# Reordering y, the gates and the reloads, sharing the opening between ScalarE and VectorE, spreading the FFN gate passes, and moving g by 64 bytes

## What is computed

```
h = x + RMSNorm_post(W_out [GLA(xn) ; SSD(xn)]),  xn = RMSNorm_pre(x)
y = h + RMSNorm_post(ConvFFN(RMSNorm_pre(h)))
D_MODEL = 2048; FFN_DIM = 5632; GLA_HEADS = 4; SSD_HEADS = 16

def _conv_ffn(xn, s_ffn, p):
    u = xn @ p['ffn_w_in']
    u, buf = _causal_dwconv(u, s_ffn, p['ffn_conv_w'], p['ffn_conv_b'])
    a, b = jnp.split(u, 2, axis=-1)
    return (jax.nn.silu(a) * b) @ p['ffn_w_out'], buf.astype(xn.dtype)

# in _mixer, once W_in has made q, k, v, g, lr, z, xbc, dt:
    lg = jax.nn.log_sigmoid((lr @ p['gla_w_gate2'] + p['gla_b_gate']).astype(f32)) / GLA_GATE_NORMALIZER
    ...
    y = y.reshape(B, L, SSD_GROUPS, SSD_WIDTH // SSD_GROUPS) * jax.nn.silu(
        z.reshape(B, L, SSD_GROUPS, SSD_WIDTH // SSD_GROUPS).astype(f32))
    y = _rmsnorm(y, p['ssd_norm'].reshape(SSD_GROUPS, SSD_WIDTH // SSD_GROUPS)).reshape(B, L, SSD_WIDTH)
```

## Time and profile before

| what | us |
| --- | --- |
| median of 3 runs | 2804.49 |
| lowest and highest | 2802.88, 2816.77 |
| the profiled execution's own time | 2808.16 |
| its span, first to last instruction | 2806.4 |
| PE busy in the span | 2719.0 |
| granted TensorE clock, mean | 0.983 |
| opening, input projection and recurrences | about 0 to 960 |
| FFN, 22 blocks | about 1045 to 2760 |

### The profile page before, as it was taken

The page is one execution under the profiler, slowest core; times in us unless marked ns, Lnnn a source line. Parts: engine busy times, 40 slices in busy tenths (PEclk is TensorE's granted clock), DMA queues, the critical chain, the costliest instruction groups (busy, mean ns, idle before and its releaser), DMA issues.

```text
span 2806.4 us, 48458 instructions
## 1 busy us (share of the span) xinstructions
PE 2719.0 (97%) x20078; PEld 2675.7 (95%) x20078; DVE 1280.7 (46%) x1462; ACT 744.0 (27%) x1198; POOL 1077.7 (38%) x466
## 2 busy tenths in 40 slices
PE   7999999899999988999999999999999999999996
PEld 6999999799989977999999999999999999999996
DVE  7544544555126346533443444443344434444436
ACT  3322222423103224322222222222222222222222
POOL 5333222323223345443443434443443434344337
PEclk9999999899999989999999999999999999999998
DMA  4222246412343423222222223222222222222224
GB/s 157 88 82 94 78 163 194 162 60 64 131 164 115 150 68 111 91 77 89 76 88 78 84 83 91 83 76 83 76 88 78 83 83 76 90 88 80 76 85 166
DMA packets 84595, 277.00 MB, mean 99 GB/s; under 512 B 9024, under 2 KB 13760, under 8 KB 83536
## 3 DMA queue, kind: packets, MB, share of 16 engines
q1 hardware_dynamic: 56160, 207.12, 23.7%
q10 hardware_dynamic: 28272, 67.35, 6.7%
HBM read 242.79 MB, written 31.65 MB: 98 GB/s over the span
## 4 chain that ended last, share of the span: by engine, by line
PE 69%; issue 19%; POOL 7%; DVE 4%; ACT 0%; DMA 0%; POOLq 0%; DVEq 0%; ACTq 0%
PE psum_proj L894 26%; PE psum_work L894 18%; PE psum_proj L897 13%; PE psum_work L897 9%; POOL w_lo L354 5%; DVE arena L1813 2%; POOL arena L389 1%; DVE x_lo L1341 1%; PE psum_work L1021 1%; POOL arena L406 1%; DVE x_hi L1339 1%; DVE arena L1836 1%; PE psum_work L1016 0%; POOL arena L397 0%; PE psum_work L981 0%
## 5 line engine op out<-in xcount | busy, mean ns | idle before, releaser
L354 POOL TENSOR_TENSOR w_lo<-raw,w_hi 128x1024 fp32r<-128x1024 f32 x386 | 988.1, 2571 | 1673.9 <-ACT w_hi L416 1673.9
L894 PE MATMUL psum_proj<-x_hi,w_hi 128*128 128x288 f32 (+2 forms) x3104 | 880.3, 302 | 32.2 <-POOL w_lo L354 11.5
L894 PE MATMUL psum_proj<-x_lo,w_hi 128*128 128x288 f32 (+2 forms) x3104 | 891.8, 298 | 0.0
L897 PE MATMUL psum_proj<-x_hi,w_lo 128*128 128x288 f32 (+2 forms) x3104 | 669.5, 297 | 0.0
L894 PEld LDWEIGHTS psum_proj<-x_hi,w_hi 128*128 128x128 f32 x3104 | 597.2, 192 | 51.6 <-issue 23.1
L416 ACT ACTIVATE w_hi<-raw 128x1024 fp32r<-128x1024 f32 x386 | 395.0, 1050 | 793.8 <-PE psum_proj L897 520.2
L894 PEld LDWEIGHTS psum_proj<-x_lo,w_hi 128*128 128x128 f32 x3104 | 594.1, 191 | 2.7 <-issue 1.9
L897 PEld LDWEIGHTS psum_proj<-x_hi,w_lo 128*128 128x128 f32 x3104 | 515.7, 190 | 0.0
L894 PE MATMUL psum_work<-x_lo,w_hi 128*128 128x256 f32 (+1 forms) x1408 | 407.0, 296 | 0.0
L894 PE MATMUL psum_work<-x_hi,w_hi 128*128 128x256 f32 (+1 forms) x1408 | 387.0, 297 | 0.7 <-POOL w_lo L354 0.7
L897 PE MATMUL psum_work<-x_hi,w_lo 128*128 128x256 f32 (+1 forms) x1408 | 302.4, 296 | 0.0
(11 more groups left out here) (298 smaller groups left out, 3267.9 us busy)
## 6 DMA issues: line engine op xcount, KB each, us to landing
raw<-in_weights_dram SPq DMA_DIRECT2D x386, 512.0 KB, 3.5
spill<-tail ACTq DMA_DIRECT2D x24, 288.0 KB, 2.1
arena<-in_xT_dram SPq DMA_DIRECT2D x4, 1152.0 KB, 11.3
y_spill<-arena ACTq DMA_DIRECT2D x4, 1152.0 KB, 9.2
h_spill<-arena ACTq DMA_DIRECT2D x1, 4608.0 KB, 14.5
x_hi<-h_spill ACTq DMA_DIRECT2D x1, 4608.0 KB, 17.5
out_yT_dram<-arena ACTq DMA_DIRECT2D x8, 576.0 KB, 3.6
arena<-in_ssdT_in_dram ACTq DMA_DIRECT2D x8, 512.0 KB, 5.7
```

The source lines that it names most:

```text
L354: nc.gpsimd.tensor_tensor(w_lo[:, slot], raw[:, r], w_hi[:, slot].bitcast(F32), ALU.subtract).then_inc(lo_ready, 1)
L894: nc.tensor.matmul(banks[:, n, 0:b - a], w_hi[:, slot, k], (hi, lo)[part][:, a:b], start=first and part == 0, stop=False)
L897: mm = nc.tensor.matmul(banks[:, n, 0:b - a], w_lo[:, slot, k], hi[:, a:b], start=False, stop=last)
```

## The change

Four parts.

1. **Opening.** ACT makes `x_hi` (with the weight vector as its scale) and then the square, for each slice; DVE makes `x_lo` and adds the squares in pairs; POOL has no part in it beside `weight_lo`. PE sums eight pairs over partitions, and from slice 8 on it also works tile 1, slice by slice behind tile 0. The load of the masks moves behind slice 7, and ACT rounds unit 4 before the root.
2. **y, gates, reloads.** ACT rounds the first half of y before it takes the gate logits and the second half right behind them, all in m = 32. exp and ln stand in m = 33, both low halves go out in m = 34, and in m = 35 the two loads of q and k are issued ahead of the two high halves. DVE's steps of the gates go one half tile earlier.
3. **FFN.** DVE's two taps are parted, and the four steps stand behind down tiles 1, 3, 6 and 9. ACT rounds two weight units before `g_hi`, not after.
4. **Memory.** A tensor `apart` of 64 bytes a partition stands ahead of `tail`, `g_hi` and `g_lo`. They begin at 209,792, a multiple of 128.

```diff
+        sb("apart", [P, 16])
         with nc.sbuf_tensor("tail", [P, 4736], F32) as tail:
...
-        xsum = A(14336, T)
+        xsq = [A(11008 + T * i, T) for i in range(4)]
...
             for kt in range(KT):
+                x = xin[kt // 4][:, kt % 4 * T:(kt % 4 + 1) * T]
                 act.wait_ge(x_in[min(kt // 4, 2)], 32 if kt >= 8 else 16)
-                if kt >= 2:
-                    act.wait_ge(sq_used if kt % 2 else sq_sum, kt // 2)
-                nc.scalar.activation(stage[:, kt % 2], xin[kt // 4][:, kt % 4 * T:(kt % 4 + 1) * T],
-                                     ACT.Square).then_inc(sq_ready, 1)
+                nc.scalar.activation(x_hi[:, kt], x, ACT.Copy, scale=V("mix_pre", kt)).then_inc(x_hi_w, 1)
+                if kt >= 4:
+                    act.wait_ge(sq_used, kt // 2 - 1)
+                nc.scalar.activation(xsq[kt % 4], x, ACT.Square).then_inc(sq_ready, 1)
...
+            def y_high(g):
+                for j in range(4 * g, 4 * g + 4):
+                    act.wait_ge(ymix, j + 1)
+                    nc.scalar.activation(y_hi[:, j], XC[:, j], ACT.Copy).then_inc(yhi, 1)
...
                 if m == GAP_GATE:
-                    gates()
-                if m in (GAP_YNORM + 2, GAP_YNORM + 3):
-                    g = m - GAP_YNORM - 2
                     for j in range(2):
                         act.wait_ge(hs_out[j], 16 * BATCHES // 2)
-                    for j in range(4 * g, 4 * g + 4):
-                        act.wait_ge(ymix, j + 1)
-                        nc.scalar.activation(y_hi[:, j], XC[:, j], ACT.Copy).then_inc(yhi, 1)
-                if m == GAP_YNORM + 3:
-                    y_low_out(0)
+                    y_high(0)
+                    gates()
+                    y_high(1)
+                if m == GAP_GATE + 1:
...
-                    load_over_y(0)
-                    y_high_out(0)
-                    load_over_y(1)
-                    y_high_out(1)
+                if m == GAP_GATE + 3:
+                    for g in range(SG):
+                        load_over_y(g)
+                    for g in range(SG):
+                        y_high_out(g)
...
-            def ffn_down(unit, half_unit):
+            def ffn_down(unit, half_unit, blk, q):
 
                 two_hi(unit, half_unit, 2)
+                high_of(2 * blk + 1, q, 1)
                 two_hi(unit + 2, half_unit + 1, 0)
...
+            for kt in range(KT):
+                pe.wait_ge(x_split, kt + 1)
+                mm = kt_of(0, kt)
+                if kt == 7:
+                    mm.then_inc(units_done, 1)
+                if kt >= 8:
+                    if kt == KT - 1:
+                        mm.then_inc(units_done, 1)
+                    mm = kt_of(1, kt - 8)
                 if kt % 2:
-                    pe.wait_ge(sq_ready, kt + 1)
-                    sum_tokens([stage[:, 1]], 0, sq_used, kt == 1, False)
+                    pe.wait_ge(sq_sum, kt // 2 + 1)
+                    sum_tokens([xsq[(kt - 1) % 4]], 0, sq_used, kt == 1, kt == KT - 1)
...
-                    if d in (1, 4, 7):
-                        block_end(blk, q, (1, 4, 7).index(d))
+                    if d in (1, 3, 6, 9):
+                        block_end(blk, q, (1, 3, 6, 9).index(d))
```

More of the change, by code:

```diff
@@ L357, in _ @@
             weight_lo(0, 0, 0)
[L359 to L366, removed]
+            weight_lo(1, 1, 1)
             def weights_lo(start, stop):
@@ L818, in ffn_up, with high_of @@
                             .then_inc(f_silu, 1)
-                        act.wait_ge(f_prod, pair + 1)
-                        nc.scalar.activation(g_hi[:, q, j // 2], fgate, ACT.Copy).then_inc(f_hi, 1)
-            def ffn_down(unit, half_unit):
+                        if first or j == 1:
+                            high_of(pair, q, j // 2)
+            def high_of(pair, q, i):
+                act.wait_ge(f_prod, pair + 1)
+                nc.scalar.activation(g_hi[:, q, i], fgate, ACT.Copy).then_inc(f_hi, 1)
+            def ffn_down(unit, half_unit, blk, q):
                 two_hi(unit, half_unit, 2)
+                high_of(2 * blk + 1, q, 1)
                 two_hi(unit + 2, half_unit + 1, 0)
@@ L927, in sum_tokens, with kt_of @@
                 mm.then_inc(done, 1)
-            def x_arrives(kt):
-                if kt % 2:
-                    pe.wait_ge(sq_ready, kt + 1)
-                    sum_tokens([stage[:, 1]], 0, sq_used, kt == 1, False)
-                pe.wait_ge(x_split, kt + 1)
-            pe.wait_ge(setup, 2)
-            project(0, 0, 0, 0, before=x_arrives)
-            pe.wait_ge(sq_sum, KT // 2)
-            sum_tokens([xsum], 0, sq_used, False, True)
-            with pe.Fori(0, XBC_TILES // 2) as i:
+            def kt_of(tile, kt):
+                slot = 2 * tile + kt // 8
+                if kt % 8 == 0:
+                    pe.wait_ge(lo_ready, slot + 1)
+                return products(slot, kt % 8, tile, (HALF, 256)[tile], kt == 0, kt == KT - 1, x_hi[:, kt], x_lo[:, kt])
+            pe.wait_ge(setup, 2)
+            pe.wait_ge(taken, 2)
+            for kt in range(KT):
+                pe.wait_ge(x_split, kt + 1)
+                mm = kt_of(0, kt)
+                if kt == 7:
+                    mm.then_inc(units_done, 1)
[3 more added lines that the diff above has]
+                    mm = kt_of(1, kt - 8)
+                if kt % 2:
+                    pe.wait_ge(sq_sum, kt // 2 + 1)
+                    sum_tokens([xsq[(kt - 1) % 4]], 0, sq_used, kt == 1, kt == KT - 1)
+            mm.then_inc(units_done, 1)
+            for kt in range(8, KT):
+                mm = kt_of(1, kt)
+            mm.then_inc(units_done, 1)
+            project(2, 4, 0, 0, 256)
+            with pe.Fori(1, XBC_TILES // 2) as i:
                 pair(i, split=256)
@@ L1342, in _ @@
                     .then_inc(x_split, 1)
+                if kt % 2:
+                    ve.wait_ge(sq_ready, kt + 1)
+                    tt_op(xsq[(kt - 1) % 4], xsq[(kt - 1) % 4], xsq[kt % 4], ALU.add).then_inc(sq_sum, 1)
             ve.wait_ge(masks_in, 16)
```

47 lines of the change are left out of this document (26 added, 21 removed).

## The result

| | us |
| --- | --- |
| before, median of 4 runs | 2809.94 (2802.88 to 2816.77) |
| after, median of 4 runs | 2769.06 (2764.26 to 2770.59) |
| ratio of the times | 0.986, 95% interval 0.9839 to 0.9882 |
| profiled execution, before and after: span | 2806.4 and 2768.2 |

The changed kernel is 1.4% faster. The forecast was 2768.8. One more run of before came with this comparison, so its median is 2809.94 here and not 2804.49; from span to span the gain is 38.2 us, where 35.7 had been summed.

What follows compares the result with a forecast made beforehand. TensorE, busy 2719.0 of 2806.4 us, was taken as the bound, leaving its idle time, lower clock and pace. -7.5 - 9.5 - 8.2 - 10.5 = -35.7 took the median from 2804.5 to 2768.8; range 2761 to 2781.

Steps and rivals of the forecast that it cites:

- Opening: Before tile 2: tile 1's work fills the holes where tile 0 waited for slices; -7.5 us, from -6 to -9.5.
- The root and the reciprocal: Opening, for tile 2's buffer: start at 42.5, end before 48.9, hidden by tile 1's second half; otherwise they would cost 5 us.
- The sum: Opening, the four programs laid against each other: tile 2 at 48.9 us, 8.0 earlier, with some 3 us of DVE waits.
- y, gates, reloads: Gates to first attention step: 10.8 us less, the gates' 2.3 included, less 1.3 for the clock; -9.5, from -5 to -12.5.
- The landing: Both loads of q and k before the first attention step: land at 548 us on the old clock, bounds 542.5 and 551.2.
- the step itself: First attention step: four heads in 1.9 us, PE back at the main matmuls at 550.4 instead of 561.2.
- the 1.3 taken off for the clock: First attention step: 1.3 us of the gain given up, for a clock that may fall in the wait of 2.7 us.
- the gates: Gate logits: ACT rounds four slices of y first, so PE returns to the main matmuls 2.3 us later.
- The low halves: y's low halves: out at 530 us behind exp and ln, landing at 534.6 and about 537.5; the loads wait for these.
- FFN passes: FFN down tiles: parted taps remove the wait in full, 21 x 0.39 us; -8.2, from -6 to -8.5.
- g by 64 bytes: FFN, g at a multiple of 128 bytes: 4224 matmuls 2.5 ns shorter each; -10.5 us, from -9.5 to -11.5.
- The first rival: FFN: the place of g changes nothing, so the sum is -25.2 and the time 2779.3 us; chance 13%.

Runs made afterwards that it cites:

- e5: The kernel before with the opening change alone; 2800.97 us, ratio 0.9976 to the kernel before.
- e12: The changed kernel with 192 bytes instead of 64 ahead of tail and g; 2770.62 us, ratio 0.9889 to the kernel before.
- e14: The changed kernel without the 64 bytes ahead of tail and g; 2779.97 us, ratio 0.993 to the kernel before.
- e6: The kernel before with the y, gates and reloads change alone; 2797.54 us, ratio 0.9971 to the kernel before.
- e10: The changed kernel with y's low halves and the two loads issued one half tile earlier each; 2773.58 us, ratio 0.9874 to the kernel before.
- e4: The kernel before with the FFN change alone (taps parted, g_hi behind two weight units); 2797.55 us, ratio 0.9971 to the kernel before.
- e2: The kernel before with 128 bytes ahead of tail, g_hi and g_lo; 2804.13 us, ratio 0.9996 to the kernel before.
- e3: The kernel before with 64 bytes ahead of the arena, moving gla_ops, tail and g; median 2800.14 us, ratio 0.998; second execution, a single run, 2805.16.
- e13: e3 with three matmuls of 8 columns added at the head of PE's program; 2793.08 us in a single run.
- e1: The kernel before with 64 bytes ahead of tail, g_hi and g_lo alone; 2800.94 us against 2806.62, ratio 0.9972.

## Why the prediction was right, step by step

**Opening, -7.5, measured -8.4.** The trace gives 8.4 in after, 9.1 in e5, and 7.7 to 7.8 in e12 and e14; the mean of e5's runs at full clock 8.4. PE started at 11.86 (11.95 predicted), tile 2 came near 48.4 (48.9). The root and the reciprocal hid as said: the reciprocal ends at 46.8. The sum had some 3 us of waits for DVE behind POOL; behind its first instruction PE waited for `x_lo` once in after, 0.9 us. Of the 8.4 us the sum itself had 8.0, and 0.5 were taken off.

**y, gates, reloads, -9.5, measured -7.2 in the profile, -10.0 to -10.2 in the traces of e6, e12 and e14, and -9.3 +- 1.8 in the runs of e6.** The landing was right. With the 15.9 us added that after was ahead before the gates, its loads land at 548.0 on the old clock (548 predicted), PE arrives at 545.6 (545.3), and the wait is 2.4 us (2.7).

Two terms were mis-sized. The first is the step itself: the prediction has PE back at the main matmuls 2.4 us after 548, with four heads in 1.9 us as "its usual pace". The usual pace is that of before's next step, 3.73 us for the same 32 matmuls (timeline of PE in before):

```profile
574.52 3.73 PE L1050 MATMUL psum_work<-arena 128*128 128x128 f32 x32
```

The step takes 4.35 us at full clock (e6, e12, e14) and 5.83 in after. So the gain there was over-counted by 2.0 us, and the 1.3 taken off for the clock hid part of it. That clock came in after alone (the 32 matmuls took 5.29 us, and 3.81 in e6, e12 and e14). The second is the gates. Their wait grew by 2.4 us as said, in after and in e6, but what PE lost by it was 2.5 us in after, 1.4 in e6 and e14 and 1.1 in e12. The stretch at clock 0.50 lasted 13.7 us in after and 10.2 in before and in the three others, where more of it fell into the longer wait and less on the main matmuls. That after's 2.5 meets the 2.3 is luck.

The low halves went out late, as the prediction said, and e10, which issues them and the loads one half tile earlier each, has no wait left.

**FFN passes, -8.2, measured -7.5.** The wait is gone in full, as said. The term was mis-sized: the prediction took 0.39 us a block, while the earlier trace rows has 7.6 us in all, 21 times 0.36, and e4's FFN is shorter by 7.5.

**g by 64 bytes, -10.5, measured -10.3** (after against e14, FFN to FFN). The first rival, that the place does nothing, falls. The prediction's reason was too simple, though: it took a multiple of 128 bytes as the whole cause, since two tensors off it agreed to 0.1 ns. A third place off it gave 133.2 in its one trace (e2), and `gla_ops` on it went at both paces (e3, e13).
By the Trainium skill, TensorE: Matmul & The Clock Gate, Back-to-back issue gap, an isolated matmul of 288 columns follows another after 122.5 ns at every one of these places. The prediction left out that the same section keeps this rule for isolated matmuls and has the spacing in a stream set by the weight loads too, and here each matmul has its own. No run here came to 122.5; the means of g and `gla_ops` with the same 288 columns span 131.4 to 134.4.

**The parts are not quite independent.** Part 4 without part 3 loses 4.0 us to a longer wait; part 3 takes that away. The sum was right because it was made for all four together: 7.5 + 10.3 = 17.8 in the FFN. At full clock the four parts alone give 6.1 + 7.2 + 8.4 + 5.1 = 26.8 +- 1.4 us, 30.8 with these 4.0, and the runs of after 28.2 +- 0.8 against the 35 of before; the 2.6 us between are under twice their error and stay open.

**What the sum had left out** is the clock of the stretches that the change doesn't touch: +7.7 and -3.2 us in this pair of profiles, up to 20.5 and 51.2 us at the lower level in others. In the profile the four parts gave 8.4 + 7.2 + 17.8 = 33.4 us of the 35.7, and the untouched stretches 4.5 more. Means over the runs, before 2807.0 (35 runs) or 2809.9 (the 4 above) and after 2768.2, make the gain 38.7 to 41.6 us, more than the 35.7 predicted; against the 9 runs of before on the third chip, 2803.0, it would be 34.8, and on which chip the four runs of after were made is not on record. The four runs of after lost 37.3 us to the clock, and before 48.1. How much of this difference the change brings (4.2 +- 1.9 in e6, mostly the half of the attention's wait that stood at the lower level) and how much is chance in four runs stays open. So the mechanisms and the size of the gain were foreseen, but a median within 0.3 us of the forecast is luck.

## What to carry to other kernels

- Before the gain of a faster engine is counted, look at the wait behind it: 11.7 us of pace were 7.5 us of time until DVE's passes had been spread over the tiles.
- An idle time of 12 us cost more than its length here, since the engine came back at the lower clock: 1.7 us more for the step behind it. One of 2.4 us did so in one trace, and waits of 2.2 to 2.3 us did not in three others.
- Count the records of a step in the trace before giving it a length: four heads are 32 records and 3.7 us, not 1.9.
- Where single runs differ by 20 us through the granted clock, span times clock tells edits of 5 us which the times alone leave unclear, as long as PE isn't idle at the lower level. The trace's own stretches tell smaller ones, but the FFN differed by 2.3 us without an edit to it (before and e5), and by 3.7 between two executions of e3.

## What the runs showed of the hardware

- A matmul of 288 columns of fp32r follows the last after 131.4 to 134.4 ns. Moving operand at a multiple of 128 bytes: 131.4 to 132.3 (g), 131.7 or 134.4 (`gla_ops`, by the program). 64 bytes past one: 134.0 to 134.4, or 133.2 in one trace of another place.
- The same kernel in two executions, on two chips: g at 132.3 and 131.4 ns.
- Three matmuls of 8 columns at the head of PE's program (e13) moved the pace of 256 columns in the input projection from 118.3 to 115.9 ns, and `gla_ops` from 131.7 to 134.4.
- 32 matmuls of 128 columns in float32 took 3.7 to 3.8 us at the upper clock (before, e6), and 5.55 us when they began at the lower (before).
- The granted clock in the stretch with matmuls of 8 columns (370 to 490 us) was at its lower level for 0 to 20.5 us, for the same instructions in before, e1 to e4 and e6; between 735 and 875 us for 17.1 to 51.2.
